# The values of the differential attention as seven half-size products, in both layers

## What is computed

```python
h = rms_norm(x, norm1_g) * (1 + sc1) + sh1                 # 512 tokens x 1024
cq, ckv, kr, glu, dq, dk, dv, gates = split_cols(h @ w_in)  # dv: 512 columns
# values of the differential attention, 4 heads of 128:
v = dv.reshape(b, s, DIFF_HEADS, 2 * DIFF_HD)
p = softmax(q1 @ k1) - lam * softmax(q2 @ k2)
o = p @ v
# beside it: latent attention (q and keys turned by rope_2d) and
u = a * sigmoid(g); u = depthwise_conv(u, 31 taps) + conv_b
```

## Time and profile before

| | layer 0 | layer 1 |
|---|---|---|
| PE on `dv` (four tiles) | 189.4 to 216.9 us | 997.0 to 1024.5 us |
| PE's first attention product | 217.56 us | 1025.14 us |
| DVE's convolution ends | 195.6 us | 1002.9 us |
| DVE idle ahead of the first scores | 17.68 us | 18.32 us |
| POOL done with `rotate` 3 | 205.6 us | 1013.0 us |

### The profile page before, as it was taken

How to read it: one execution, slowest core, us unless ns; L and a number is a source line. 1 busy time by engine, 2 the same in 40 slices (tenths; PEclk the granted TensorE clock), 3 DMA queues, 4 the chain that set the end, 5 groups by cost and what they waited for, 6 DMA issues and landing times.

```text
span 1468.3 us, 19532 instructions
## 1 busy us (share of the span) xinstructions
PE 1386.8 (94%) x7590; PEld 819.1 (56%) x7590; DVE 799.1 (54%) x1758; ACT 368.1 (25%) x803; POOL 209.9 (14%) x146
## 2 busy tenths in 40 slices
PE   5999999999999999989997979999999999999886
PEld 3444447754444445655554537744668885666553
DVE  2679954778887953533131118894763443434333
ACT  4112414532223012222221224141542202100001
POOL 0220524200011210012221210152000110000000
PEclk9999999999999999999999998999999999999899
DMA  9412220144535447299999968232533478999996
GB/s 379 166 36 89 83 77 38 59 158 161 183 100 201 161 192 320 102 343 419 417 419 420 415 264 347 94 115 77 202 123 144 162 303 361 401 420 420 420 420 260
DMA packets 59551, 347.66 MB, mean 237 GB/s; under 512 B 8388, under 2 KB 15172, under 8 KB 28352
## 3 DMA queue, kind: packets, MB, share of 16 engines
q1 hardware_dynamic: 53856, 335.86, 57.8%
q0 software_dynamic: 5024, 8.40, 1.5%
q10 hardware_dynamic: 576, 2.10, 0.4%
HBM read 343.44 MB, written 11.80 MB: 242 GB/s over the span
## 4 chain that ended last, share of the span: by engine, by line
PE 84%; DMA 6%; DVE 4%; SPq 3%; ACT 2%; issue 1%; DVEq 0%; POOLq 0%; ACTq 0%
PE bank L467 79%; DMA arena<-w_up_in 5%; ACT arena L1335 2%; PE bank L834 2%; SPq L3061 2%; PE bank L567 1%; DVE arena L1818 1%; PE bank L1209 1%; DMA x<-x_in 1%; DMA arena<-y 0%; PE bank L1229 0%; DVE am L2104 0%; SPq L3109 0%; SPq L3095 0%; DVE arena L2209 0%
## 5 line engine op out<-in xcount | busy, mean ns | idle before, releaser
L467 PE MATMUL bank<-arena 128*128 128x512 f32 (+10 forms) x5912 | 1194.6, 437 | 23.3 <-DMA arena<-w_up_in 12.9
L467 PEld LDWEIGHTS bank<-arena 128*128 128x128 f32 (+4 forms) x5912 | 655.6, 161 | 484.1 <-issue 360.4
L1335 ACT ACTIVATE arena<-bank 128x512 f32<-128x512 f32 (+5 forms) x423 | 200.7, 494 | 904.6 <-PE bank L467 805.0
L1818 DVE SCALAR_TENSOR_TENSOR arena<-arena,bank 64x256 f32<-64x256 f32 (+2 forms) x121 | 57.9, 479 | 247.7 <-ACT arena L1335 182.3
L1818 DVE SCALAR_TENSOR_TENSOR arena<-arena,early 128x512 f32<-128x512 f32 (+1 forms) x254 | 177.6, 773 | 0.4
L2104 DVE TENSOR_REDUCE am<-bank 128x1 f32<-128x512 f32 (+1 forms) x96 | 55.5, 599 | 107.8 <-PE bank L467 107.6
L2879 POOL TENSOR_TENSOR arena<-arena 128x512 f32<-128x512 f32 (+1 forms) x32 | 37.3, 1166 | 368.4 <-DVE arena L1818 368.4
L1335 ACT ACTIVATE arena<-bank,am 128x512 f32<-128x512 f32 (+1 forms) x96 | 58.6, 613 | 80.8 <-DVE am L2107 80.6
L2918 POOL DMA_INDIRECT y<-arena,routing x33 | 32.9, 998 | 181.2 <-ACT arena L1335 181.2
L834 PEld LDWEIGHTS bank<-con,arena 128*128 128x128 f32 x240 | 29.9, 141 | 26.1 <-issue 11.9
L834 PE MATMUL bank<-con,arena 128*128 128x128 f32 x240 | 38.6, 275 | 5.1 <-DVE arena L2119 4.6
(11 more groups left out here) (242 smaller groups left out, 929.4 us busy)
## 6 DMA issues: line engine op xcount, KB each, us to landing
arena<-w_gate_in SPq DMA_DIRECT2D x60, 1024.0 KB, 22.0
arena<-w_up_in SPq DMA_DIRECT2D x60, 1024.0 KB, 24.5
arena<-w_down_in SPq DMA_DIRECT2D x45, 1024.0 KB, 22.8
arena<-mg_in SPq DMA_DIRECT2D x12, 2048.0 KB, 8.0
arena<-adaT_in SPq DMA_DIRECT2D x40, 512.0 KB, 3.6
arena<-adaT_in SPq DMA_DIRECT2D x16, 1024.0 KB, 7.1
arena<-ada_in SPq DMA_DIRECT2D x6, 2048.0 KB, 15.5
arena<-mo_in SPq DMA_DIRECT2D x6, 2048.0 KB, 7.8
```

Of the source, the lines that this page charges most:

```text
L467: return nc.tensor.matmul(out, w, rhs, start=start, stop=stop)
L1335: return nc.scalar.activation(out, in_, fn, **kw)
L1818: return V.scalar_tensor_tensor(out, in0, sc, in1, op0=op0, op1=op1)
```

## The change

The product of 512 tokens by 1024 channels by 512 columns is cut into quarters of each operand (`w11`: first four channel blocks and first 256 columns, `w12`: last four channel blocks and first 256 columns, `w21`, `w22`: the same for the last 256 columns; `h` into context or latent tokens by first or last four channel blocks). Eight quarter products become seven, of sums of quarters:

- **PE.** Seven products `q`, `x`, `r`, `11`, `12`, `y`, `z`, each two tiles of 128 tokens by four channel blocks by 256 columns into one bank. `q` and `x` are banks that ACT evicts, the other five are evicted by DVE. `x`, `r`, `12`, `y` wait for a sum of weights by POOL. Ahead of the attention PE waits for one sum more (`corner`).
- **POOL.** Sums of the weights in the ring slot: `s1` (`w21 += w22`) and `s2` right after `rotate` 2, `s4` once `q` is done (it overwrites `w11`), `s3` once `x` is done. Sums of the results: `u` (`v12 = v21 - v22`) once DVE has evicted `r`, `corner` (`v22 = v21 + v22`) once it has evicted `y`. `sums_ahead(0, 0)` now stands between `s3` and `u`, `rotate` 3 between `u` and `corner`, `add_channels` behind `corner`.
- **POOL in layer 1.** The four sums of token blocks (`token_sums`), which only layer 0 had, are made there too, behind the addition for the norm.
- **DVE.** Five additions or subtractions, each of two blocks of 256 columns, out of a bank and SBUF into `vd`: `r`, `11`, `12` (behind `u`), `y`, `z` (behind `corner`). They stand behind `swapped_sin` of the keys.
- **ACT.** Two evictions (`q`, `x`) in place of four.
- Signs of the token sums are turned round, so that in the gates of layer 0 a few additions become subtractions and one three-operand instruction becomes a subtraction; their number stays the same.

```diff
-                for t in range(4):
-                    ps = begin("a", ("dv", l, t))
-                    for k in range(KD):
-                        last = mm(ps[:, :], h[:, k, t * 128:t * 128 + 128], w[:, k, :], k == 0, k == KD - 1)
-                    end("a", last)
+                pe.wait_ge(sums_ready, pool_sums("tokens", l, 0))
+                for name, cls, cols, toks, needs in (("q", "a", w11, h[:, 0:4, 0:CTX], None), ("x", "a", w21, h_sums[0], "s1"),
+                                                     ("r", "d", wide_sum, h_sums[1], "s2"), ("11", "d", w12, h[:, 4:8, 0:CTX], None),
+                                                     ("12", "d", w11, h[:, 4:8, CTX:T], "s4"), ("y", "d", w21, h_sums[2], "s3"),
+                                                     ("z", "d", w22, h_sums[3], None)):
+                    ps = begin(cls, (name, l, "dv", 0))
+                    if needs:
+                        pe.wait_ge(sums_ready, pool_sums(needs, "dv", l))
+                    for t in range(2):
+                        for k in range(4):
+                            last = mm(ps[:, 256 * t:256 * t + 256], toks[:, k, 128 * t:128 * t + 128], cols[:, k, :], k == 0, k == 3)
+                    end(cls, last)
...
                 pe.wait_ge(s["pool_set"], seen(l, "pool_set", 2))
+                pe.wait_ge(sums_ready, pool_sums("corner", "dv", l))
...
                 swapped_sin(Pd, kd, 3, 2)
+                ps = take(("r", l, "dv", 0))
+                dve.wait_ge(empty["a"], A[("q", l, "dv", 0)])
+                give(V.tensor_tensor(v21, v11, grid(ps[:, :], 2), op=ADD))
+                ps = take(("11", l, "dv", 0))
+                give(V.tensor_tensor(v11, v11, grid(ps[:, :], 2), op=ADD))
+                ps = take(("12", l, "dv", 0))
+                dve.wait_ge(sums_ready, pool_sums("u", "dv", l))
+                give(V.tensor_tensor(v12, v12, grid(ps[:, :], 2), op=ADD))
+                ps = take(("y", l, "dv", 0))
+                give(V.tensor_tensor(v21, grid(ps[:, :], 2), v21, op=SUB))
+                ps = take(("z", l, "dv", 0))
+                dve.wait_ge(sums_ready, pool_sums("corner", "dv", l))
+                give(V.tensor_tensor(v21, v21, grid(ps[:, :], 2), op=ADD))
...
+                if l == 1:
+                    pool.wait_ge(empty["a"], A[("n1", 1, 1, 0)])
+                    pool.wait_ge(empty["d"], Dn[("n1", 1, 1, 1)])
+                    token_sums()
+                    pool.wait_ge(sums_ready, pool_sums("tokens", 1, 0))
...
-                rotate(3, (0, 128), kd, Pd, "cos_d", None, HD)
...
+                G.tensor_tensor(w21, w21, w22, op=ADD).then_inc(sums_ready, 1)
+                pool.wait_ge(sums_ready, pool_sums("s1", "dv", l))
+                G.tensor_tensor(wide_sum, w11, w21, op=ADD).then_inc(sums_ready, 1)
+                pool.wait_ge(sums_ready, pool_sums("s2", "dv", l))
+                pool.wait_ge(full["a"], A[("q", l, "dv", 0)])
+                G.tensor_tensor(w11, w12, wide_sum, op=ADD).then_inc(sums_ready, 1)
+                pool.wait_ge(full["a"], A[("x", l, "dv", 0)])
+                G.tensor_tensor(w21, wide_sum, w22, op=SUB).then_inc(sums_ready, 1)
+                pool.wait_ge(sums_ready, pool_sums("s3", "dv", l))
+                if l == 0:
+                    sums_ahead(0, 0)
+                pool.wait_ge(empty["a"], A[("x", l, "dv", 0)])
+                pool.wait_ge(empty["d"], Dn[("r", l, "dv", 0)])
+                G.tensor_tensor(v12, v21, v22, op=SUB).then_inc(sums_ready, 1)
+                rotate(3, (0, 128), kd, Pd, "cos_d", None, HD)
+                pool.wait_ge(empty["d"], Dn[("y", l, "dv", 0)])
+                G.tensor_tensor(v22, v21, v22, op=ADD).then_inc(sums_ready, 1)
...
-                if l == 0:
-                    sums_ahead(0, 0)
```

More of the change, by code:

```diff
@@ L1511, in _ @@
                 ada_raw(("dk", l, 0))
-                for t in range(4):
-                    ps = take(("dv", l, t))
-                    give(f(vd[:, t, :], ps[:, :], ACT.Copy))
+                ps = take(("q", l, "dv", 0))
+                give(f(v11, grid(ps[:, :], 2), ACT.Copy))
+                ps = take(("x", l, "dv", 0))
+                give(f(v22, grid(ps[:, :], 2), ACT.Copy))
                 ada_raw(("dv", l, 0))
@@ L2226, in group_tile @@
                         dve.wait_ge(empty["a"], A[("q", l, b, g)])
-                        give(V.tensor_tensor(t2[:, 0:256], t1[:, 0:256], ps[:, 0:256], op=SUB))
+                        give(V.tensor_tensor(t2[:, 0:256], t1[:, 0:256], ps[:, 0:256], op=ADD))
                     elif p == 3:
@@ L2236, in group_tile @@
                         ps = take(("y", l, b, g))
-                        give(stt(t2[:, 0:256], ps[:, 0:256], -1.0, t2[:, 0:256], MUL, SUB))
+                        give(V.tensor_tensor(t2[:, 0:256], ps[:, 0:256], t2[:, 0:256], op=SUB))
                     elif p == 6:
```

58 lines of the change are left out of this document (36 added, 22 removed).

## The result

The changed kernel took 1481.94 us (median of 6 runs, 1480.86 to 1483.2), the kernel before 1468.76 beside it (6 runs, 1464.31 to 1472.09): a ratio of 1.0075, 95% interval 1.0055 to 1.0096, or some 13 us slower by the medians and 11 by the ratio. The prediction was 1481. The profiled execution of after took 1482.02 us with a span of 1480.1; before it was 1470.08 and 1468.3.

What follows compares the result with a forecast made beforehand. PE's products bound the projections' ends; with the change, POOL's sums queue with DVE's convolution. 3.9 (layer 0) + 6.4 (layer 1) + 3.0 (clock) = 13.3 us later: 1483.4 us profiled, 1481 on the median, range 1470 to 1487.

Steps and rivals of the forecast that it cites:

- A: The forecast itself: POOL's sums queue with DVE's convolution; 1475 to 1486 us, chance 0.71.
- Taking turns: POOL sums and DVE convolution instructions never run at once, so times add; two instructions of about 2.9 us behind `rotate` 2.
- Layer 0: End of the projections: attention starts at 221.4 us against 217.56, 3.9 us later.
- The string's part up to `swapped_sin`: Layer 0: six POOL sums push the end of `swapped_sin` from 200.62 us by 11.94 to 212.56.
- `z` and the banks: Layer 0: `z` waits for the bank of `r`, 210.1 to 213.3 us, at no cost while `corner` is later.
- Token sums: Layer 1: four new POOL sums delay DVE by 5.3 us; PE waits 2.4 us ahead of `uq`.
- B: Rival: layer 1's token sums slip into the reciprocals and the 5.3 us go; 1472.5 to 1475.5 us, chance 0.12.
- End of layer 1: Convolution ends at 1017.6 us, attention starts at 1031.5 against 1025.14: 6.4 us later.
- The clock: PE at half clock around each attention's start: 1.5 us a layer between bounds 0 and 3.0, 3.0 us in all.
- Shifts go through: Later phases and their transfers start from PE events, so a shift goes through to the end.
- The term for the layers: Delays at the projections' ends: 3.9 us in layer 0 and 6.4 us in layer 1.
- C: Rival: sums hide in DVE's 17.68 and 18.32 us of waiting; 3.3 us won per layer, 1461 us, chance 0.09.

Runs made afterwards that it cites:

- e7: Kernel before with four more POOL sums of 128x1024 behind `rotate` 2 in each layer, for which no product waits; 1469.34 us, ratio 1.0002.
- e6: Changed kernel with layer 1's four token sums behind the copy of `kr` instead of behind the norm's addition; 1484.29 us, ratio 1.0099.
- e3: Changed kernel with products nobody reads filling PE's waits ahead of `z` and of the attention in both layers; 1474.79 us, ratio 1.0055.
- e10: Kernel before with each `dv` tile made of nine products instead of eight in both layers; 1473.68 us, ratio 1.0029.
- e4: Changed kernel with POOL's four weight sums 2 columns wide instead of 256, so values are wrong; 1504.39 us in one execution.
- e5: Change in layer 0 only, `swapped_sin` and evictions ahead of the last 16 convolution instructions, `rotate` 3, `u`, `corner` ahead of `sums_ahead`; 1473.59 us, ratio 1.003.
- e12: The kernel of e9 run once more, in more rounds; 1465.95 us, ratio 0.9985 against the kernel before.
- e8: Changed kernel with the weight sums on DVE and new orders on POOL and, in layer 1, on DVE; 1469.37 us, ratio 0.9996 to before.
- e9: e8 with layer 1's token sums on DVE too, two and two ahead of `glu_up(2)` and `glu_up(3)`; 1467.77 us, ratio 0.9991 to before.

## Why the prediction was right

The time and the mechanism came out as forecast (A); single terms were off in both directions.

- **Taking turns.** Right, and the two instructions of about 2.9 us are there (2.83, twice, in layer 0; 2.56 and 2.57 in layer 1). The price was the sum's own 2.35 us; the runs give 2.09 us a sum (e7: 8.4 us for four; after: 4.2 us for two in layer 0, and 18.96 - 10.58 = 8.4 us for four in layer 1). So "never run at once" was a little too strong: some 0.3 us of each sum cost DVE nothing.
- **Layer 0.** Forecast 3.9 us later, measured 2.4. The string's part up to `swapped_sin` was put at 11.94 us and took 10.1: 4.2 for `s1` and `s2`, 5.9 in `swapped_sin` (10.85 us in place of 4.91). `s4` was kept out from 192.99 us to the end of the row, as the norm's addition in the earlier trace rows. Behind it `r`, `u`, `rotate` 3, `corner`, `z` ran as worked out.
- **`z` and the banks.** Right: 1.38 us of wait for `r`'s bank, with no cost of its own, since the eviction of `z` waited 4.85 us for `corner` all the same.
- **Token sums.** Forecast 5.3 us of DVE delay; the norms were done at 958.27 us instead of 953.15, 5.1 us later, of which 0.8 is the layer's later start on this scale and 4.3 DVE's delay: three hold-ups of 2.09 us less the 1.74 us of idle time. The wait ahead of `uq` was 1.44 us and not 2.4 for that. B did not come about: the sums got in first. What B's place, among the reciprocals, would have cost is not shown; e6's place lies behind them, in the convolution again, and cost more.
- **End of layer 1.** Forecast 6.4, measured 4.6 (1030.60 less the layer's 0.84 less 1025.14). The four weight sums cost the convolution 8.4 us, not 9.40; `s4` and `s3` got into the row this time (2.49 us from 1003.15, 2.40 from 1006.54), so that the forecast's way of adding them held, at the lower price.
- **The clock.** Under-sized: 1.5 us a layer was taken between bounds of 0 and 3.0; it cost 2.3 and 2.9 to 3.1 us (ladder; e3). The row it was scaled from the earlier trace rows has 6.1 us of work at half clock, and here it was 4.9 us in layer 0 and some 6.5 behind the wait in layer 1, in spite of the shorter idle time.
- **Shifts go through.** Not contradicted inside the program, as the ladder shows, where the profiled execution of before is what changed pace. e10 leaves open whether a part of it is lost.

The term for the layers was 3.3 us too high (10.3 against 7.0), the clock 2.2 to 2.4 us too low (3.0 against 5.2 to 5.4): 13.3 forecast, 12.2 us by the ladder. That the sum came so near the 13 us measured by the medians (11.0 by the ratio) is in part luck of two errors with opposite signs.

- **C.** The reason given against it was the right one: the idle time lies behind the end of `swapped_sin`, and the sums are wanted before. e7 shows that four sums alone do hide, and e4 that short sums leave PE as the bound. Whether POOL's sums could be hidden by another order stays open: e5's order didn't do it, but left DVE idle for 5.5 us ahead of two evictions. The Trainium skill (SBUF — State Buffer, "Summary: rules for kernel authors") has the second one of such a meeting block fully until the first finishes. The runs agree as far as 2.09 of 2.35 us; `s4` of layer 0, though, waited for a whole row of DVE instructions and not for one (8.94 us).

## What to carry to other kernels

An engine that waits is not free capacity for its neighbour: where two engines hold each other up as here, count each of the helper's instructions as time of the other engine too, and ask what on the critical path stands behind that engine's row. Here it was cheaper to give the sums to the engine that seemed the busy one (1.22 us of its own against 2.09 us taken from it); together with the new orders this turned 0.75% slower into level, or 0.15% faster at best (e12, whose interval ends at 1.000). Before a shift is called absorbed, look at whether kernels that come in early move by the same amount: the one profile that all are compared with may be the odd one.

## What was not expected of the hardware

- POOL doesn't always get the next turn. A sum that followed POOL's last one by 0.8 to 0.9 us got into DVE's row (layer 1 of after, 1003.15 us, 2.49, and 1006.54, 2.40); one that came 9.72 us after it was kept out for the rest of the row (192.99 us, 8.94), and so were two of 128x8 in e4 (191.26 us, 2.64, 13.93 us after; 995.97 us, 4.89, 5.00 us after, in the same kind of row as the two that got in). POOL's own pause doesn't decide it alone: `s4` of e5 came 9.71 us after POOL's last one and took 2.95 us (191.76 us), amid `swapped_sin`. What decides it was not tried.
- A POOL sum of 128x1024 took 2.35 us alone, 2.41 beside DVE instructions of 128x256 and 2.68 beside those of 128x512; the hold-up of DVE was 2.09 us with both.
- The clock fell to 0.50 inside the waits of 4.7 us (after, layer 0) and 5.2 us (e5), for 6.8 and 10.2 us; beside the single wait of 2.7 us in layer 1 of e8 it stayed at the upper level. The length of the wait alone doesn't tell: in e9 and e12, two runs of one kernel with a single wait of 1.8 us there, the clock was at 0.50 for 3.4 us, from 1.8 us into that attention in e9 and from 6.8 us in e12.
